# Decoder trunk step: one loop for three heads, sample mask built on VectorE, first transposes and loads of the attention moved forward

## The chip, the cores and the metric

The kernel runs on one core of one Trainium2 chip. The metric is the device time of one execution in microseconds (us). PE is the matrix engine (TensorE), DVE is VectorE, ACT is ScalarE, POOL is GpSimd and SP is SyncE, which here only issues DMAs.

## What is computed

One inference step of a two-layer decoder trunk, in float32, for a prompt (2048 tokens, width 1024) and for 8 sample sequences of 4 new tokens each with 2048 cached tokens. Both share the weights.

```python
# layer 0: gated linear attention (4 heads, dk 128, dv 256), chunks of 64 tokens
q, k, v, g, lr = split(rmsnorm(x) @ w_in)
log_a = log_sigmoid(lr @ w_a2 + b_a) / 16          # per token and key channel
b     = cumsum(log_a, within a chunk)
o     = tril((q*exp(b)) @ (k*exp(-b)).T) @ v + (q*exp(b)) @ S
S     = exp(b_last) * S + (k*exp(b_last - b)).T @ v
h     = x + (rmsnorm(o) * silu(g)) @ w_out
# layer 1: stick-breaking attention (16 heads of 64) on K, V made once from h
z     = q @ k.T / 8 + bias
w     = sigmoid(z) * product over later keys of (1 - sigmoid(z)), strictly causal
h     = h + ((w @ v) * silu(gate)) @ w_out2 ;  y = rmsnorm(h)
```

The outputs are y for both groups, the final states S, and K and V of all new tokens.

## The kernel before

The kernel is a row of stages, each a block in which every engine runs its own program and meets the others through semaphores; between blocks all engines meet. In order: the first projection (`proja`), the GLA stage (`gla`), its output projection (`outa`), the second projection (`projb`), the attention of the prompt (`att`), and the attention of the sample together with the last projection (`smp`).

**GLA.** The four heads follow one another. A head has 16 tiles of 128 prompt tokens and one tile of 32 sample tokens. The decay factors of the next head are made beside the tiles of the current one, in four spans of 512 tokens: PE multiplies `lr` by `w2` (L782, "logit"; L786 for the sample's 32 columns), DVE adds the bias (L945), DVE and ACT make the log-sigmoid (L953 to L957), DVE scans it into `b_sum` (L966), and so on. `order` is the list of the steps of a head; the first span's logit stands in its third tile. `first` is the list of what precedes head 0 and also makes head 0's factors. `over_heads` runs `first`, then heads 0 and 1 in a hardware loop with `h` in a register, then head 2 and head 3 written out, head 3 without the steps for a next head. `w2` and `bias` have one buffer each, so `gate_weights(h)` (L637) may only load them for a head when the fifth logit of the head before is copied (`logit_cp`). SP loads them for head 1 before its loop, and in head h, after the spans of the next head and three stores of `o`, those for head h+2 (L670 to L672). After that come the state store, the sample states out and in, two more stores of `o` and `sums` (L684).

The masks are made once. POOL sets and cuts `keep`, `tok_mask`, `row_mask`, `mask_work` and `smp_work` with affine selects (L973 to L1002). DVE casts `mask_work` and `smp_work` into the integer masks `may` and `may_smp` (L934, L935), which the predicated copies of the scores use (L881, L883). `smp_work` says which of the 32 sample tokens may look at which: the same sequence, and not later.

**Attention.** It goes over 8 pairs of heads, each in five phases, and in beats: `attention_schedule` writes the order out by hand, and every engine follows the same list. A "z" item makes the scores of one tile of queries for one head (PE), two sigmoids (ACT, L1638 and L1646), a product scan (DVE, L1688) and a product (POOL, L1721). The "first" phase puts two such items in each of beats 0 to 7, over 128 to 512 keys; from beat 8 one item of 1024 keys stands in a beat. An "a" item, from beat 11, transposes weights and multiplies by V. A "turn" item transposes 512 raw columns of K and of V (PE, L1612), copies K out (ACT, L1653) and V (DVE, L1697), and lets SP load the next raw tile and store K (L1471, L1522). `raw_k`, `raw_v` and `k_tok` have two buffers each, so turn m+2 needs what turn m has freed. For pair 0 the four turns stand at beats 7 to 10, for later pairs at beats 40 (pair - 1) + 12, +14, +16 and +18. With the turns of pair 0 SP also issues loads that are needed later: the K of span 3 and the Q of span 1, the Q of span 3, the K of pair 1 (8 transfers), and the sample inputs (`new.load`: page table, bias, and tokens in pieces of 128 bytes).

Of the kernel before, what the change touches and what calls it, by code (L numbers as in the profile page):

```python
# [24 lines left out]
ALU = mybir.AluOpType  # L25
# [7 lines left out]
P = 128  # L33
# [3 lines left out]
NSEQ, TSEQ = 8, 4  # L37
SMP = NSEQ * TSEQ
# [478 lines left out]
def gla(nc, c, projT, w_alpha2, b_alpha, state_in, state_prompt, state_sample, o_out, sums, early):  # L517
# [8 lines left out]
    with ExitStack() as stack:  # L526
# [23 lines left out]
        mask_work, smp_work = s.sb("mask_work", [P, P]), s.sb("smp_work", [SMP, NSEQ, TSEQ])  # L550
# [46 lines left out]
        def over_heads(engine, run):  # L597

            run(START, first)
            with engine.Fori(0, GH - 2) as h:  # L600
                run(h, order)
            run(GH - 2, order)
            run(GH - 1, [x for x in order if x[1] == 0])
# [23 lines left out]
        def _(sp):  # L627
# [31 lines left out]
            sp.wait_ge(logit_cp, 5)  # L659
            gate_weights(1)  # L660

            def run(h, is_last):
                for u in range(NCH):
                    if not is_last:

                        sp.wait_ge(o_mm, h * n_tiles + (n_tiles if u == NCH - 1 else 4 * u + 4))
                        span(h + 1, u)
                    if u < NCH - 1:
                        store_o(h, u)
                if not isinstance(h, int):  # L670
                    sp.wait_ge(logit_cp, h * 5 + 10)
                    gate_weights(h + 2)  # L672
# [12 lines left out]
            with sp.Fori(0, GH - 2) as h:  # L685
                run(h, False)
            run(GH - 2, False)
# [5 lines left out]
        def _(pe):  # L693
# [3 lines left out]
            def run(h, items):  # L697
# [52 lines left out]
                def sample():  # L750
# [10 lines left out]
                    pe.wait_ge(logit_cp, h * 5 + (5 if isinstance(h, int) and h == GH - 1 else 10))  # L761
# [103 lines left out]
        def _(dve):  # L865
# [7 lines left out]
            def run(h, items):  # L873
# [49 lines left out]
                for kind, off, *x in items:  # L923
# [8 lines left out]
                    elif kind == "masks":  # L932
                        dve.wait_ge(masks, 16)
                        dve.tensor_copy(may[:, :], mask_work[:, :]).then_inc(prep, 1)  # L934
                        dve.tensor_copy(may_smp[:, :], smp_work[:, :, :].rearrange("p s n -> p (s n)")).then_inc(prep, 1)  # L935
                        dve.wait_ge(prep, 6)
                    elif kind in ("logit", "logit_smp", "abs", "decay", "scan"):
# [22 lines left out]
                        else:  # L960
                            dve.wait_ge(log_sigmoid, span_no)
                            if h is START and u == 0:
                                dve.wait_ge(masks, 8)
# [7 lines left out]
        def _(pool):  # L971
# [6 lines left out]
            pool.memset(smp_work[:, :, :], 1.0).then_inc(masks, 1)  # L978
            pool.wait_ge(masks, 6)
# [12 lines left out]
            pool.affine_select(out=smp_work[:, :, :], in_=smp_work[:, :, :], compare_op=ALU.is_ge, fill=0.0,  # L992
                               base=0, pattern=[[-TSEQ, NSEQ], [0, TSEQ]], channel_multiplier=1).then_inc(masks, 1)
            pool.wait_ge(masks, 12)
            pool.affine_select(out=smp_work[:, :, :], in_=smp_work[:, :, :], compare_op=ALU.is_ge, fill=0.0,
                               base=0, pattern=[[TSEQ, NSEQ], [1, TSEQ]], channel_multiplier=-1).then_inc(masks, 1)
# [317 lines left out]
def attention_schedule():  # L1314
# [19 lines left out]
    def put(beat, item):  # L1334
        beside.setdefault(beat, []).append(item)
# [4 lines left out]
    for pair in range(PAIRS):  # L1340
        for m in range(4):
            put(7 + m if pair == 0 else 40 * (pair - 1) + LAG + 1 + 2 * m, ("turn", pair, m))
# [14 lines left out]
def prompt_attention(nc, c, projT, parts, b_sb, k_out, v_out, oT, new):  # L1357
# [48 lines left out]
    with ExitStack() as stack:  # L1406
# [34 lines left out]
        def _(sp):  # L1441
# [51 lines left out]
            load_first_k(1, 0, 4)  # L1493
            load_gate(0)
            for kind, pair, *x in order:
# [9 lines left out]
                elif kind == "turn":  # L1505
# [7 lines left out]
                    if pair == 0 and m == 0:  # L1513
                        load_first_k(3, 0, 4)
                        load_q(0, 1)
                    elif pair == 0 and m == 1:
                        load_q(0, 3)
                    elif pair == 0 and m == 2:
                        load_k(1)
                    elif pair == 0:  # L1520
                        new.load(sp)
# [828 lines left out]
```

## Time and profile before

| | |
|---|---|
| time, three runs | 3374.26 us median (3369.12 to 3375.23) |
| the profiled execution | 3375.23 us, span of its instructions 3373.6 us |
| PE busy | 3159.3 us, 94% of the span |
| DVE, ACT, POOL busy | 1661.7, 1398.5, 887.3 us |
| granted TensorE clock, mean | 0.969 of full speed |
| GLA stage | about 626 to 886 us |
| prompt attention | about 1888 to 2872 us |

An engine can only be late through its own queue: it works off its instructions in order, and one that waits holds all behind it. The busy share of PE says how much of the span could be taken from it at best; the waits in front of its instructions say where it stands.

### The profile page before, as it was taken

How to read it: one execution, taken by the hardware profiler on the slowest of the kernel's cores; microseconds unless marked ns; L12 is line 12 of the kernel's file. 1: busy time of each engine (PE TensorE's matmuls, PEld its weight loads, DVE VectorE, ACT ScalarE, POOL GpSimd, SP SyncE). 2: the span in 40 equal slices, each digit the busy share in tenths (PEclk: the TensorE clock that was granted, in tenths of full speed). 3: DMA queues.
4: the chain of work that ended last, by engine and by line, in shares of the span. 5: the costliest groups of instructions: out<-in, count | busy, mean ns of one | idle time of the engine just before them, and what ended most of it. 6: DMA issues, size and time to landing. Idle time of an engine off the chain costs nothing. (4 is left out here: it accounts for less than half of the span.)

```text
span 3373.6 us, 49748 instructions
## 1 busy us (share of the span) xinstructions
PE 3159.3 (94%) x17836; PEld 2480.2 (74%) x17836; DVE 1661.7 (49%) x1965; ACT 1398.5 (41%) x2330; POOL 887.3 (26%) x936
## 2 busy tenths in 40 slices
PE   6999999799799699999999589999999999799998
PEld 6999999556588599999999455555555555566665
DVE  5111122387444422112222288998999898443442
ACT  5111111365311221112211278888888787344442
POOL 0000000255111000000000256776767676000000
PEclk9999999799899899999999689999999999899999
DMA  4122111455254545213431455343433410899995
GB/s 152 57 75 75 69 57 58 165 180 184 101 175 147 178 158 181 76 68 133 175 101 44 135 162 136 77 125 113 110 97 100 126 32 20 348 323 375 368 336 212
DMA packets 253345, 489.74 MB, mean 145 GB/s; under 512 B 27181, under 2 KB 137490, under 8 KB 240850
## 3 DMA queue, kind: packets, MB, share of 16 engines
q1 hardware_dynamic: 228402, 350.61, 32.0%
q0 software_dynamic: 24752, 136.63, 11.3%
q8 instruction: 115, 1.88, 0.2%
q14 instruction: 76, 0.62, 0.1%
HBM read 329.58 MB, written 157.59 MB: 144 GB/s over the span
## 5 line engine op out<-in xcount | busy, mean ns | idle before, releaser
L1721 POOL TENSOR_TENSOR att_w<-att_w,att_rest 128x1023 f32<-128x1023 f32 (+7 forms) x384 | 614.7, 1604 | 303.1 <-DVE att_rest L1688 291.0
L469 PE MATMUL projb_acc<-projb_x_hi,projb_w_hi 128*128 128x416 f32 x1280 | 452.1, 353 | 25.9 <-DVE projb_x_lo L459 25.8
L469 PE MATMUL projb_acc<-projb_x_hi,projb_w_lo 128*128 128x416 f32 x1280 | 450.1, 352 | 0.0
L469 PE MATMUL projb_acc<-projb_x_lo,projb_w_hi 128*128 128x416 f32 x1280 | 449.6, 351 | 0.0
L1549 PEld LDWEIGHTS att_wT_acc<-const_ident,att_w 128*128 128x128 f32 x2176 | 237.0, 142 | 210.4 <-issue 153.1
L1638 ACT ACTIVATE att_rest<-att_z,att_bias 128x1024 f32<-128x1024 f32 (+7 forms) x384 | 332.9, 867 | 84.7 <-PE att_z L1595 36.4
L1688 DVE TENSOR_TENSOR_SCAN att_rest<-att_rest,att_zero 128x128 f32<-128x128 f32 (+7 forms) x256 | 355.0, 1402 | 22.9 <-ACT att_rest L1638 22.9
L292 PE MATMUL proja_acc<-proja_x_hi,proja_w_hi 128*128 128x416 f32 x1000 | 354.3, 354 | 0.8 <-DVE proja_x_lo L265 0.7
L292 PE MATMUL proja_acc<-proja_x_hi,proja_w_lo 128*128 128x416 f32 x1000 | 352.1, 352 | 0.0
L292 PE MATMUL proja_acc<-proja_x_lo,proja_w_hi 128*128 128x416 f32 x1000 | 350.3, 350 | 0.0
L1549 PE MATMUL att_wT_acc<-const_ident,att_w 128*128 128x128 f32 x2176 | 315.1, 281 | 31.1 <-ACT att_k_tok L1653 14.6
L1646 ACT ACTIVATE att_w<-att_z,att_bias 128x1024 f32<-128x1024 f32 (+7 forms) x384 | 331.9, 864 | 0.0
L1563 PE MATMUL att_o_acc<-att_wT,att_v_tok 128*64 128x512 f32 (+3 forms) x1280 | 305.3, 556 | 6.8 <-DVE att_silu L1706 5.9
L1688 DVE TENSOR_TENSOR_SCAN att_rest<-att_rest,att_carry,att_zero 128x1024 f32<-128x1024 f32 x128 | 299.2, 2337 | 7.1 <-ACT att_rest L1638 7.0
L418 ACT ACTIVATE projb_out<-projb_acc 128x416 f32<-128x416 f32 x160 | 83.1, 519 | 501.7 <-PE projb_acc L469 501.7
L230 ACT ACTIVATE proja_out<-proja_acc 128x416 f32<-128x416 f32 x125 | 64.5, 519 | 484.4 <-PE proja_acc L292 484.4
L469 PEld LDWEIGHTS projb_acc<-projb_x_hi,projb_w_hi 128*128 128x128 f32 x1280 | 241.2, 188 | 29.3 <-issue 19.6
L469 PEld LDWEIGHTS projb_acc<-projb_x_lo,projb_w_hi 128*128 128x128 f32 x1280 | 241.4, 189 | 3.2
L469 PEld LDWEIGHTS projb_acc<-projb_x_hi,projb_w_lo 128*128 128x128 f32 x1280 | 241.8, 189 | 2.2
L1676 DVE COPY att_wT<-att_wT_acc 128x512 f32<-128x512 f32 (+2 forms) x320 | 192.7, 602 | 93.1 <-PE att_wT_acc L1549 90.4
L1591 PE MATMUL att_z<-att_k,att_q_hi 128*128 128x512 f32 (+3 forms) x640 | 226.9, 420 | 0.4 <-ACT att_w L1646 0.4
L506 POOL DMA_DIRECT2D proj_b<-projb_out x32 | 17.1, 533 | 710.7 <-ACT projb_out L418 535.0
(256 smaller groups left out, 5066.4 us busy)
## 6 DMA issues: line engine op xcount, KB each, us to landing
smp_k_pages<-in_cache_k SPq DMA_DIRECT2D x128, 512.0 KB, 7.1
smp_v_pages<-in_cache_v SPq DMA_DIRECT2D x128, 512.0 KB, 7.2
proj_b<-projb_out POOLq DMA_DIRECT2D x32, 1040.0 KB, 4.4
proj_a<-proja_out POOLq DMA_DIRECT2D x24, 1040.0 KB, 4.5
kq_hi<-projb_slab POOLq DMA_DIRECT2D x16, 1024.0 KB, 6.0
kq_lo<-projb_slab POOLq DMA_DIRECT2D x16, 1024.0 KB, 8.9
att_q_hi<-kq_hi SPq DMA_DIRECT2D x60, 256.0 KB, 4.2
att_q_lo<-kq_lo SPq DMA_DIRECT2D x60, 256.0 KB, 5.1
```

The costliest lines, as they stand in the source:

```text
L230: act.activation(out[:, b, at:at + size], acc[:, q, 0:size], ACT.Sigmoid if gate else ACT.Copy).then_inc(copied, 1)
L292: mm = pe.matmul(acc[:, q, 0:size], w[:, b, k, :], x[:, k, at:at + size], start=(k == 0 and w is w_hi and x is x_hi), stop=(k == KD - 1 an ...
L418: act.activation(out[:, b, at:at + size], acc[:, q, 0:size], ACT.Sigmoid if kind == "gate" else ACT.Copy).then_inc(copied, 1)
L469: mm = pe.matmul(acc[:, q, 0:size], w[:, b, k, :], x[:, k, at:at + size], start=(k == 0 and w is w_hi and x is x_hi), stop=(k == KD - 1 an ...
L1549: mm = pe.transpose(wT_ps[:, h, (t % 4) * P:(t % 4 + 1) * P], weight(pair, phase, h, t, at, P), c.ident[:, :])
L1563: pe.matmul(o_ps[h * HD:(h + 1) * HD, lo:BANK], v_tok[:, pair % 2, j, h * HD:(h + 1) * HD], wT[:, h, n % 2, lo:BANK], start=(j == 4 * g + ...
L1591: pe.matmul(z_ps[:, n % 2, at:end], q_hi[:, t // 4, h, tile].bitcast(F32R), k2[:, pair % 2, h, lo + at:lo + end].bitcast(F32R), start=carr ...
L1638: act.activation(rest[:, n % n_rest, 1024 - size:1024], z_ps[:, n % 2, 0:size], ACT.Sigmoid, bias=bias[:, 1, head:head + 1], scale=-HD ** ...
L1646: act.activation(weight(pair, phase, h, t, 0, size), z_ps[:, n % 2, 0:size], ACT.Sigmoid, bias=bias[:, 0, head:head + 1], scale=HD ** -0.5 ...
L1676: dve.tensor_copy(wT[:, 1, n % 2, lo:BANK], wT_ps[:, 1, lo:BANK]).then_inc(copied[1], 1)
L1688: dve.tensor_tensor_scan(passing, passing, zero[:, 0:1].broadcast_to([P, size]), carry_of(t, h) if carried else rest[:, n % n_rest, 1024:1 ...
L1721: pool.tensor_tensor(these, these, passed[:, 1:size], ALU.mult).then_inc(w_made, 1)
```

## The change

There are three edits to the GLA stage and one to the attention. In GLA, the hardware loop now covers heads 0 to 2, and `gate_weights` for head h+1 is issued at the start of head h, for every head; `smp_work` and its selects are gone from POOL and `may_smp` is made on DVE from `tok_mask`, `row_mask` and `may`; the scan of the first span waits for all masks. In the attention, the turns of pair 0 stand at beats 4 to 7 and the loads that went with them are issued before the list begins.

```diff
         def over_heads(engine, run):
             run(START, first)
-            with engine.Fori(0, GH - 2) as h:
+            with engine.Fori(0, GH - 1) as h:
                 run(h, order)
-            run(GH - 2, order)
             run(GH - 1, [x for x in order if x[1] == 0])
...
             early.load(sp)
-            sp.wait_ge(logit_cp, 5)
-            gate_weights(1)
             def run(h, is_last):
+                if not is_last:
+                    sp.wait_ge(logit_cp, h * 5 + 5)
+                    gate_weights(h + 1)
                 for u in range(NCH):
...
-                if not isinstance(h, int):
-                    sp.wait_ge(logit_cp, h * 5 + 10)
-                    gate_weights(h + 2)
                 sp.wait_ge(s_made, h * NCK + NCK)
...
-            with sp.Fori(0, GH - 2) as h:
+            with sp.Fori(0, GH - 1) as h:
                 run(h, False)
-            run(GH - 2, False)
             run(GH - 1, True)
...
-                    pe.wait_ge(logit_cp, h * 5 + (5 if isinstance(h, int) and h == GH - 1 else 10))
+                    pe.wait_ge(logit_cp, h * 5 + (5 if isinstance(h, int) else 10))
...
                     elif kind == "masks":
-                        dve.wait_ge(masks, 16)
+                        dve.wait_ge(masks, 13)
                         dve.tensor_copy(may[:, :], mask_work[:, :]).then_inc(prep, 1)
-                        dve.tensor_copy(may_smp[:, :], smp_work[:, :, :].rearrange("p s n -> p (s n)")).then_inc(prep, 1)
+
+                        dve.wait_ge(prep, 5)
+                        dve.tensor_tensor(ke_smp[:, :, 0:SMP], tok_mask[0:SMP, :, :],
+                                      row_mask[:, :].unsqueeze(2).broadcast_to([SMP, NSEQ, SMP]), ALU.mult).then_inc(prep, 1)
                         dve.wait_ge(prep, 6)
+                        dve.tensor_reduce(mask_work[0:SMP, 0:SMP], ke_smp[:, :, 0:SMP].rearrange("p s n -> p n s"),
+                                      mybir.AxisListType.X, ALU.add).then_inc(prep, 1)
+                        dve.wait_ge(prep, 7)
+                        dve.tensor_tensor(mask_work[0:SMP, SMP:2 * SMP], mask_work[0:SMP, 0:SMP], may[0:SMP, 0:SMP],
+                                      ALU.mult).then_inc(prep, 1)
+                        dve.wait_ge(prep, 8)
+                        dve.tensor_copy(may_smp[:, :], mask_work[0:SMP, SMP:2 * SMP]).then_inc(prep, 1)
+                        dve.wait_ge(prep, 9)
...
                             if h is START and u == 0:
-                                dve.wait_ge(masks, 8)
+                                dve.wait_ge(masks, 13)
...
-            pool.memset(smp_work[:, :, :], 1.0).then_inc(masks, 1)
-            pool.wait_ge(masks, 6)
+            pool.wait_ge(masks, 5)
...
-            pool.affine_select(out=smp_work[:, :, :], in_=smp_work[:, :, :], compare_op=ALU.is_ge, fill=0.0,
-                               base=0, pattern=[[-TSEQ, NSEQ], [0, TSEQ]], channel_multiplier=1).then_inc(masks, 1)
-            pool.wait_ge(masks, 12)
-            pool.affine_select(out=smp_work[:, :, :], in_=smp_work[:, :, :], compare_op=ALU.is_ge, fill=0.0,
-                               base=0, pattern=[[TSEQ, NSEQ], [1, TSEQ]], channel_multiplier=-1).then_inc(masks, 1)
+            pool.wait_ge(masks, 10)
...
-            put(7 + m if pair == 0 else 40 * (pair - 1) + LAG + 1 + 2 * m, ("turn", pair, m))
+            put(4 + m if pair == 0 else 40 * (pair - 1) + LAG + 1 + 2 * m, ("turn", pair, m))
...
             load_raw(0, 0)
             load_raw(0, 1)
             load_first_k(1, 0, 4)
+            load_first_k(3, 0, 4)
             load_gate(0)
+            load_q(0, 1)
+            load_q(0, 3)
+            load_k(1)
+            new.load(sp)
...
-                    if pair == 0 and m == 0:
-                        load_first_k(3, 0, 4)
-                        load_q(0, 1)
-                    elif pair == 0 and m == 1:
-                        load_q(0, 3)
-                    elif pair == 0 and m == 2:
-                        load_k(1)
-                    elif pair == 0:
-                        new.load(sp)
```

## Rows read from the trace of the kernel before

**Rows 1.** Windows of busy time: stretch, length, busy per engine, clock, DMA share, GB/s.
```profile
626.00:886.00 260.00, 237.48 (x1284) 140.04 (x1284) 182.91 (x382) 134.18 (x373) 124.12 (x104) 0.91 0.53 179
...
1888.00:1960.00 72.00, 36.14 (x136) 24.83 (x136) 31.53 (x33) 30.82 (x53) 25.50 (x35) 0.57 0.80 204
...
660.00:664.00 4.00, 4.00 (x12) 1.70 (x13) 1.52 (x3) 0.75 (x3) 1.26 (x1) 0.66 0.00 0
...
1915.00:1920.00 5.00, 4.24 (x12) 2.12 (x12) 3.94 (x5) 4.12 (x9) 3.86 (x6) 0.50 0.10 25
```

**Rows 2.** Timeline, GLA: start, duration, PE's logits in heads 1 and 2.
```profile
718.86 1.12 PE L782 MATMUL gla_logit_acc<-gla_rT,gla_w 16*128 16x512 f32 x2
...
776.21 1.12 PE L782 MATMUL gla_logit_acc<-gla_rT,gla_w 16*128 16x512 f32 x2
```

**Rows 3.** Line L684 (store of sums), near 718 and 775: issue, landing.
```profile
L684 SPq DMA_DIRECT2D sums<-gla_sumsq_out x1: 890/890/890, 717.9 to 717.9; - x1
DMA to landing us min/median/max: 6.0/6.0/6.0
...
L684 SPq DMA_DIRECT2D sums<-gla_sumsq_out x1: 763/763/763, 775.1 to 775.1; - x1
DMA to landing us min/median/max: 5.6/5.6/5.6
```

**Rows 4.** Tile gla_w, whole span: from issue to landing of its four loads.
```profile
DMA to landing us min/median/max: 1.9/6.6/9.1
```

**Rows 5.** Timeline of PE in GLA: start, duration, idle before and its releaser.
```profile
659.98 1.12 PE L782 MATMUL gla_logit_acc<-gla_rT,gla_w 16*128 16x512 f32 x2 [1.55 <-DMA gla_w<-in_w_alpha]
...
766.46 0.66 PE L706 MATMUL gla_tok<-const_ident,gla_vgT 128*128 128x128 f32 x4
...
769.75 0.97 PE L706 MATMUL gla_tok<-const_ident,gla_vgT 128*128 128x128 f32 x4
...
823.91 0.66 PE L706 MATMUL gla_tok<-const_ident,gla_vgT 128*128 128x128 f32 x4
...
826.00 0.60 PE L706 MATMUL gla_tok<-const_ident,gla_vgT 128*128 128x128 f32 x4
```

**Rows 6.** Timeline, 630 to 644: the masks and what follows them.
```profile
630.02 0.14 POOL L1002 MEMSET gla_mask_work<- 64x64 f32 x1
...
636.94 0.16 DVE L935 CAST gla_may_smp<-gla_smp_work 32x32 int32<-32x32 f32 x1
...
639.43 1.60 DVE L957 SCALAR_TENSOR_TENSOR gla_logit<-gla_logit,gla_work 128x512 f32<-128x512 f32 x1 [2.33 <-ACT gla_work L842]
...
643.15 0.29 DVE L879 COPY gla_ke<-gla_kp 128x128 f32<-128x128 f32 x1 [1.45 <-PE gla_kp L714]
```

**Rows 7.** Tile gla_tok_mask: min/median/max ns, first and last start.
```profile
L891 DVE TENSOR_TENSOR gla_q_smp<-gla_qT,gla_tok_mask x4: 406/406/407, 700.5 to 867.7; 128x256 f32<-128x256 f32 x4
```

**Rows 8.** Waits, 1924.2 to 1957: us in total, times, longest.
```profile
ACT att_k_tok L1653 <- DMA out_k_prompt<-att_k_tok: 16.1, 3, 7.4
```

**Rows 9.** Timeline, 1908 to 1957: issues of SP and ACT's steps.
```profile
1908.97 0.63 SPq L1477 DMA_DIRECT2D att_silu<-proj_b  x1
...
1922.46 1.25 SPq L1465 DMA_DIRECT2D att_q_hi<-kq_hi  x2
...
1926.23 1.11 ACT L1638 ACTIVATE att_rest<-att_z,att_bias 128x1024 f32<-128x1024 f32 x1
...
1949.62 8.08 SPq L1522 DMA_DIRECT2D out_k_prompt<-att_k_tok  x1
...
1955.46 0.60 ACT L1653 ACTIVATE att_k_tok<-att_wT_acc 128x512 f32<-128x512 f32 x1 [4.93 <-DMA out_k_prompt<-att_k_tok]
1955.96 1.11 ACT L1638 ACTIVATE att_rest<-att_z,att_bias 128x1024 f32<-128x1024 f32 x1
```

**Rows 10.** The page, costliest groups: count, busy us, mean ns of one.
```profile
L1688 DVE TENSOR_TENSOR_SCAN att_rest<-att_rest,att_carry,att_zero 128x1024 f32<-128x1024 f32 x128 | 299.2, 2337 | 7.1 <-ACT att_rest L1638 7.0
```

**Rows 11.** Line L1477, 1907 to 1910: landing of the gate load.
```profile
DMA to landing us min/median/max: 7.9/7.9/7.9
```

More of the change, by code:

```diff
@@ L549, in gla @@
         may, may_smp = s.sb("may", [P, P], I32), s.sb("may_smp", [SMP, SMP], I32)
-        mask_work, smp_work = s.sb("mask_work", [P, P]), s.sb("smp_work", [SMP, NSEQ, TSEQ])
+        mask_work = s.sb("mask_work", [P, P])
         sumsq, sumsq_out = s.sb("sumsq", [P, n_tiles]), s.sb("sumsq_out", [P, n_tiles])
```

## The prediction

> **What bounds the kernel now.** I read the page's busy line first: TensorE (PE) is by far the busiest engine, so what counts is what makes it stand. The change touches only two short stretches, so next I read the windows by stage: gated linear attention (GLA, 626 to 886 us) and the first 72 us of the prompt attention [rows 1]. In the first, PE is busy 237.5 of 260 us: a wait put in front of PE there is paid in full. In the second PE is busy 36.1 of 72 us at a clock of 0.57 with the DMA engines 0.80 busy: this is a start-up bound by transfers. Then I read, around each edit, who waits for whom and when each transfer was issued and landed.
>
> **Part 1: the gate weights in GLA.** Before, SyncE issues the weights `w2` and the bias for head h+2 in the middle of head h, ahead of that head's stores. After, it issues those for head h+1 as the first thing of head h. For head 1 nothing changes. For heads 2 and 3 the load now stands behind the whole tail of the previous head: state store, sample states out and in, two stores of `o`, `sums`. The last of these, `sums`, is issued at 717.9 and at 775.1 and takes 0.9 and 0.8 us to issue [rows 3], so `w2` goes out at about 718.9 and 776.0. PE asks for it in the third tile of the head, at 718.86 and 776.21 [rows 2]. So the load leaves when it is already wanted, and every microsecond to its landing is a wait of PE, in whose queue all later matmuls of the head stand.
>
> How long is that? `sums` is only 8.5 KB and still lands 6.0 and 5.6 us after its issue, at 723.9 and 780.7 [rows 3], behind 1 MB of states each way and 0.5 MB of `o`. `w2` is next in the same queue. `w2` would follow them by a few tenths; but SyncE's tail also starts about 1 us earlier, since two issues are gone from in front of it, and some of that is kept. I take 723.9 and 780.6 for `w2` itself: 723.9 - 718.9 = 5.0 and 780.6 - 776.2 = 4.4, together 9.4 us of waiting. Bounds: 1.9 us from issue to landing, the shortest of these loads [rows 4], gives 1.9 + 1.7 = 3.6; `sums`'s own landing plus another 2 us each gives 13.4. The bias lands just behind `w2`, while the pair of matmuls runs (1.12 us [rows 2]), so VectorE's wait for it is hidden; uncovered it costs a few tenths.
>
> The Trainium skill (DMA: Bandwidth & Descriptors, Anatomy of one DMA) gives a fixed cost of about 2 us for a small transfer; by that alone the two waits would be about 4 us. The same page (Queues, rings and completion order) says descriptors of a ring are consumed in order and a completion count lands only after that engine's earlier writes; the 6.0 us of the 8.5 KB transfer agree with this.
>
> Then the clock. After a gap of only 1.55 us in front of an earlier logit matmul, the granted clock of the next 4 us was 0.66 [rows 1, 5]: PE fell to its 1.2 GHz level for a while. The price is read from one tile at either level: the first tile of head 2 takes 769.75 - 766.46 = 3.29 us in such a phase, that of head 3 takes 826.00 - 823.91 = 2.09 us at full clock [rows 5]. So 1.2 us per phase; I take 1.3 for each of two waits, 2.6 (from 0 to 2 x 2.5). Nothing later gives this back, since PE has little idle time in this stage to shrink [rows 1].
>
> **Part 2: head 2 in the loop.** The same instructions run, with one more jump back. No row prices a jump by itself, but the two heads' first logits, 57.35 us apart with an unrolled entry between them [rows 2], leave no room for a dear one either way: 0.4 us as an estimate, from 0 to 1.
>
> **Part 3: the masks.** GpSimd loses a memset and two selects, and the scan's wait for 13 instead of 8 is free, since GpSimd's last mask starts at 630.02 and VectorE casts, behind that scan, at 636.94 [rows 6]. VectorE gets five small operations where it had two, each waiting for the one before: product, reduction, product, two casts. The nearest row is a product of 128x256 at 406 ns [rows 7]; two of that size, three of 0.2 us, and the round trips between make about 2 us, up to 3.5 beside a busy GpSimd. Before, VectorE ends its casts at 637.1 and then idles 2.33 us for ScalarE and 1.45 us more before it copies the keys at 643.15 [rows 6]. That cover of 3.8 us hides it: 0. Without the cover it would cost 2 us once. What GpSimd saves is nothing either: it idles until the scan.
>
> **Part 4: the start of attention.** The turns (transposes of raw K and V) of pair 0 move from beats 7 to 10 to beats 4 to 7, and all loads that hung on them are issued in one go: the first K of span 3 (2 transfers), Q of spans 1 and 3 (8), K of pair 1 (8), and the sample inputs (table, bias, tokens). Before, ScalarE waits 16.1 us, in three pieces, for the stores of these turns [rows 8]. This looks like a prize. But turns 2 and 3 need raw tiles that are only loaded once turns 0 and 1 have freed their buffers; they now queue behind all of the list.
>
> Rate: between the issue at 1922.46 and ScalarE's release at 1955.46 there are 31 transfers of 256 KB in one queue, so about 1.0 us each after the queue filled [rows 9]. The gate load of 1908.97 landed 7.9 us later, at 1916.9 [rows 11]. After: 1916.9 + 18 = 1934.9; the sample inputs, cut in pieces of 128 bytes, add about 2.5: 1937.4. SyncE itself is held: in the before kernel the issue right behind them took 8.08 us, until 1957.75 [rows 9]. So the raw K of turn 2 leaves about 1936 and the raw V lands about 1940.3. PE meets turn 2 at about 1921 and stands until 1940; before, it did beats 7 to 10 in that time.
>
> From there: ScalarE's copy waits for the first store (1941.5), then four sigmoids of beat 7 at about 0.7 us (1.11 at twice the width [rows 9]), the copy of turn 3, and the first full-width sigmoid at 1945.4; it was at 1926.23 [rows 9]. Five such steps lie between it and the sixth: at VectorE's pace, 2.34 us for a scan [rows 10] and small copies beside it, 13.7 us with the turn. So the sixth starts at 1959.1, where it was at 1955.96 after three stalls [rows 9]: +3.1. From here before ran at half clock with gaps; a PE that has been kept busy for 14 us should not: -1.5. Sum +1.6. What comes back is the DMA engines' idle time, 0.10 busy from 1915 to 1920 where the stage's mean is 0.80 [rows 1]; what is lost is that PE no longer works in it. Bounds: raw V landing at 1934 (0.7 us a transfer) gives -5; the 8.08 us once more on top gives +9.
>
> **Sum.** 9.4 + 2.6 + 0.4 + 0 + 1.6 = +14.0 us. The profiled execution took 3375.23 (span 3373.6), 1 us over the median 3374.26. 3375.2 + 14.0 = 3389.
>
> **Rivals.** (A) Late transfers are not held by the backlog: the engines serve them beside the queued ones. Then `w2` costs 3.6 us, clock 1.2, jump 0.4, and raw V, issued at 1924, is there by 1927, which pulls the sixth step to 1945.7: -10. Sum -4.8: 3370, not slower. It decides once raw V lands before 1930. For: 0.10 DMA share at 1917. Against: an 8.5 KB transfer took 6.0 us. (B) Only the small loads slip past, or the tail of the head runs ahead, and the clock stays up: 3.6 + 0.4 + 1.6 = +5.6: 3381. (C) The scattered sample inputs hold SyncE longer than reckoned: +8 more, 3397; the 8.08 us issue speaks for it. (D) The early list drains at the higher rate: attention -5, sum +7.4: 3383.
>
> **How the numbers follow.** Forecast as summed, 3385 to 3394: 0.56. A 0.10, B 0.12, C 0.12, D 0.10. A measurement of this kernel tells about 0.2% (6.7 us) from no change: slower starts at 3381. Slower: the forecast, C, half of B and most of D, 0.80. Same: half of B, most of A, some of D, 0.14. Faster: a tail of A, 0.06. Range 3378 to 3398: it leaves out A and the tails of C.
>
> **What would show it.** In the profile after: the first logit matmul of heads 2 and 3 with about 5 us of idle, released by the DMA of `w2`, and a dip of the granted clock behind it; the GLA stage longer by some 12 us; about 1.5 to 2.5 us of mask work on VectorE with the first key copy no later; no rows of turns between 1921 and 1940 and PE idle there, released by raw K or V; DMA share near 1 from 1900 to 1946 without a gap. It is wrong if `w2` lands within 2 us, or if the turns of beat 6 do not wait.

## The result and the profile after

The change makes the kernel slower: 3396.92 us (median of 4, 3391.98 to 3398.95) against 3374.74 us (median of 4) of the kernel before on the same chip, ratio 1.0066, 95% interval 1.0049 to 1.0085. That is +22.2 us between the medians. The profiled execution took 3394.23 us with a span of 3392.6; the traces so compare at 3392.6 - 3373.6 = +19.0 us. The forecast was +14.

Where the 19.0 us lie is found by marks in both traces. The GLA stage, from its first to its last transposition of keys, takes 240.7 us in place of 221.7: +19.0. The first projection ended 2.0 us sooner, the second took 1.3 us more and the gap in front of it 1.3 us more; these and smaller differences cancel. The attention, from its first scores to its last gate, takes 976.1 us in place of 977.6. So all of it is the GLA stage. (A gate is the product L1706 of a finished piece of output with its `silu` factor; there are 32.) One trace against another is coarse: with the same GLA code the stage takes between 215.9 and 223.8 us, as the table of experiments shows. Windows of the whole stage, after (stretch, length, busy time of each engine, clock, DMA share, GB/s):

```profile
626.00:886.00 260.00, 237.06 (x1251) 139.57 (x1252) 180.60 (x372) 132.49 (x369) 119.71 (x93) 0.88 0.52 172
```

Against [rows 1] PE has the same busy time but fewer matmuls (1251 records, not 1284) and a clock of 0.88, not 0.91. That is how such a loss looks in a window: the busy share does not fall, since a matmul at half clock counts as busy for longer. The window is also fixed while the stage has grown, so it holds less of the stage's work. PE's waits in the stage from 640 us on, after (total, times, longest):

```profile
PE gla_logit_acc L778 <- DMA gla_w<-in_w_alpha: 11.7, 3, 6.3
```

PE's timeline at the first logit of heads 0, 1 and 2; they answer to [rows 5] and [rows 2]:

```profile
658.23 1.12 PE L778 MATMUL gla_logit_acc<-gla_rT,gla_w 16*128 16x512 f32 x2 [1.48 <-DMA gla_w<-in_w_alpha]
...
722.62 2.07 PE L778 MATMUL gla_logit_acc<-gla_rT,gla_w 16*128 16x512 f32 x2 [3.86 <-DMA gla_w<-in_w_alpha]
...
788.75 2.07 PE L778 MATMUL gla_logit_acc<-gla_rT,gla_w 16*128 16x512 f32 x2 [6.32 <-DMA gla_w<-in_w_alpha]
```

The two last rows had no wait before. Their own duration has gone from 1.12 to 2.07 us: the clock is down as they run. SyncE's timeline shows why the weights are late:

```profile
708.71 3.14 SPq L641 DMA_DIRECT2D gla_s_in<-in_state_gla  x1
712.11 3.15 SPq L646 DMA_DIRECT2D o_gla<-gla_o  x1
715.44 1.16 SPq L679 DMA_DIRECT2D o_gla<-gla_o_smp  x1
716.84 0.92 SPq L681 DMA_DIRECT2D sums<-gla_sumsq_out  x1
718.32 0.35 SPq L637 DMA_DIRECT2D gla_w<-in_w_alpha  x1
```

The load is issued at 718.32 and PE starts at 722.62, 4.3 us later. From issue to landing, the load itself and then the store of `sums` that stands in front of it, both heads:

```profile
DMA to landing us min/median/max: 4.2/4.5/4.8
...
L681 SPq DMA_DIRECT2D sums<-gla_sumsq_out x2: 344/630/917, 716.8 to 783.0; - x2
DMA to landing us min/median/max: 5.5/5.5/5.5
```

So `sums` lands at 722.3 and 788.5 and `w2` about 0.2 us behind it, both times.

The clock behind the first of the two long waits (2 us a window; PE's busy time is the second figure):

```profile
720.00:722.00 2.00, 0.00 (x0) 0.00 (x0) 0.00 (x0) 0.31 (x2) 1.26 (x1) 0.74 0.29 84
722.00:724.00 2.00, 1.39 (x2) 0.50 (x2) 0.00 (x0) 0.00 (x0) 0.00 (x0) 0.50 0.00 0
724.00:726.00 2.00, 2.00 (x7) 0.63 (x8) 0.75 (x1) 0.22 (x1) 0.00 (x0) 0.50 0.00 0
726.00:728.00 2.00, 2.00 (x7) 1.06 (x6) 0.96 (x2) 0.53 (x3) 0.00 (x0) 0.50 0.00 0
728.00:730.00 2.00, 2.00 (x12) 1.53 (x10) 0.43 (x3) 1.07 (x2) 0.00 (x0) 0.50 0.00 0
730.00:732.00 2.00, 2.00 (x10) 0.95 (x7) 1.12 (x3) 0.79 (x4) 1.63 (x1) 0.70 0.12 24
```

PE is busy throughout from 722.62 but at 0.50, the 1.2 GHz level, for more than 8 us. What the low clock loses is PE's busy time in a window times one minus the clock: 1.39 x 0.5 + 6 x 0.5 + 2 x 0.3 = 4.3 us. The same sum behind the wait of head 2 gives 3.7 us, together 8.0. One head can be closed to 0.1 us. From logit to logit it is 788.75 - 722.62 = 66.13 us, 8.8 more than the 57.35 of [rows 2]. Into it fall the wait of 6.32 us and the 4.3 us of clock, and out of it a phase at the low level that the kernel before had near 766 to 771, 1.7 us by the same sum: 6.3 + 4.3 - 1.7 = 8.9.

The masks, VectorE's timeline after, beside [rows 6]:

```profile
634.83 0.20 DVE L930 CAST gla_may<-gla_mask_work 128x128 int32<-128x128 f32 x1
635.07 1.25 DVE L933 TENSOR_TENSOR gla_ke_smp<-gla_tok_mask,gla_row_mask 32x256 f32<-32x256 f32 x1
636.35 0.59 DVE L936 TENSOR_REDUCE gla_mask_work<-gla_ke_smp 32x32 f32<-32x256 f32 x1
636.98 0.52 DVE L939 TENSOR_TENSOR gla_mask_work<-gla_mask_work,gla_may 32x32 f32<-32x32 f32 x1
637.53 1.17 DVE L942 CAST gla_may_smp<-gla_mask_work 32x32 int32<-32x32 f32 x1
638.74 0.69 DVE L964 SCALAR_TENSOR_TENSOR gla_logit<-gla_logit,gla_work 128x512 f32<-128x512 f32 x1
...
641.54 0.29 DVE L875 COPY gla_ke<-gla_kp 128x128 f32<-128x128 f32 x1 [1.46 <-PE gla_kp L710]
```

It is 3.9 us of work where it was 0.3. The operation that follows has no idle time in front of it, where VectorE stood 2.33 us for ScalarE, and the wait in front of the first copy of keys is what it was (1.46, before 1.45).

The attention's first turns, PE and ScalarE, and the issue that holds them:

```profile
1960.57 1.11 PE L1610 MATMUL att_wT_acc<-const_ident,att_raw_k 128*128 128x128 f32 x4 [18.69 <-DMA att_raw_k<-proj_b]
```
```profile
1962.09 0.60 ACT L1651 ACTIVATE att_k_tok<-att_wT_acc 128x512 f32<-128x512 f32 x1 [19.94 <-DMA out_k_prompt<-att_k_tok]
...
1966.12 1.11 ACT L1636 ACTIVATE att_rest<-att_z,att_bias 128x1024 f32<-128x1024 f32 x1
```
```profile
1944.58 0.59 SPq L1741 DMA_DIRECT2D new_tokens<-proj_b  x1
1945.28 12.76 SPq L1473 DMA_DIRECT2D att_raw_k<-proj_b  x1
1958.08 0.43 SPq L1473 DMA_DIRECT2D att_raw_v<-proj_b  x1
```

The attention starts 20.8 us later in this trace. In the terms of the kernel before, PE meets the third turn with its data at 1939.8 and the first full-width sigmoid stands at 1945.3.

### The profile page after: what moved, and what is told of

Same layout as the page of the kernel before. It is cut to its first block and busy times, and to the rows that moved or that the text cites. A ratio compares the mean times of both kernels' runs of the same rounds, so it can differ in the third digit from the quotient of the medians.

```text
span 3392.6 us, 50001 instructions
## 1 busy us (share of the span) xinstructions
PE 3158.6 (93%) x17836; PEld 2475.2 (73%) x17836; DVE 1664.0 (49%) x1968; ACT 1398.7 (41%) x2330; POOL 887.5 (26%) x933
## 5 line engine op out<-in xcount | busy, mean ns | idle before, releaser
L469 PEld LDWEIGHTS projb_acc<-projb_x_hi,projb_w_hi 128*128 128x128 f32 x1280 | 241.3, 188 | 32.1 <-issue 21.2
L469 PEld LDWEIGHTS projb_acc<-projb_x_lo,projb_w_hi 128*128 128x128 f32 x1280 | 241.3, 189 | 3.2
```

What stands on the lines that cost most here:

```text
L469: mm = pe.matmul(acc[:, q, 0:size], w[:, b, k, :], x[:, k, at:at + size], start=(k == 0 and w is w_hi and x is x_hi), stop=(k == KD - 1 an ...
```

## The experiments

Twelve kernels were run in four groups, each beside the kernel before on the same chip. "GLA" and the gates are from the trace of the profiled execution: the length of the stage as above, and the time from the first scores of the attention to its first and last gate. The four groups ran on different chips, so between groups the ratios compare and not the medians. The traces have noise of their own: the attention as it was before reaches its first gate after 74.3 to 77.8 us and its last after 977.5 to 981.1 (before, g1, g2, g4, g5, g6).

| kernel | median us | ratio to before, 95% | GLA | first gate | last gate |
|---|---|---|---|---|---|
| before | 3374 to 3378 | 1 | 221.7 | 74.3 | 977.6 |
| after | 3396.92 | 1.0066 [1.0049, 1.0085] | 240.7 | 74.4 | 976.1 |
| g1_loop_and_weights | 3395.14 | 1.0047 [1.0031, 1.0064] | 242.8 | 74.4 | 977.5 |
| g2_weights_at_start | 3396.70 | 1.0054 [1.0038, 1.0071] | 241.3 | 75.7 | 979.0 |
| g3_weights_back | 3380.28 | 1.0008 [0.9998, 1.0018] | 216.1 | 74.7 | 976.4 |
| g4_filler | 3393.27 | 1.0051 [1.0032, 1.0071] | 238.0 | 76.4 | 979.6 |
| g5_behind_states | 3391.34 | 1.0039 [1.0025, 1.0054] | 235.2 | 77.8 | 981.1 |
| g6_filler5 | 3394.48 | 1.0054 [1.0041, 1.0068] | 240.9 | 74.8 | 978.0 |
| a1_attention_only | 3377.01 | 1.0001 [0.9991, 1.0010] | 215.9 | 76.0 | 977.8 |
| a2_front_turns7 | 3377.36 | 1.0002 [0.9992, 1.0013] | 223.8 | 74.1 | 975.7 |
| a3_turns4_late | 3374.53 | 0.9993 [0.9983, 1.0003] | 223.5 | 58.4 | 973.1 |
| b1_spread | 3358.99 | 0.9946 [0.9933, 0.9960] | 220.2 | 59.0 | 960.8 |
| b2_spread_w2 | 3354.35 | 0.9933 [0.9921, 0.9945] | 216.7 | 58.5 | 961.8 |
| b3_masks | 3355.11 | 0.9936 [0.9920, 0.9952] | 216.8 | 60.7 | 962.3 |

**Which edit.** g1_loop_and_weights is the kernel before with the two GLA edits alone, the loop over three heads and the weights at the head's start. g2_weights_at_start leaves the loop as it was and moves only the weights:

```diff
-            sp.wait_ge(logit_cp, 5)
-            gate_weights(1)
...
             def run(h, is_last):
+                if not is_last:
+                    sp.wait_ge(logit_cp, h * 5 + 5)
+                    gate_weights(h + 1)
...
-                if not isinstance(h, int):
-                    sp.wait_ge(logit_cp, h * 5 + 10)
-                    gate_weights(h + 2)
```

> The kernel before with only the loop over heads 0 to 2 and the gate weights issued at the start of a head. Theory 1 (late weights): in the changed kernel PE waited 3.9 and 6.3 us for w2 and the period of heads 1 and 2 grew by 9.5 and 8.2 us, the rest being a half-speed clock behind each wait; so this kernel is 17 to 19 us slower than before, about 3392. Theory 2 (the GLA edits explain only their waits, about 10 us, and the rest of the loss sits in the masks or the attention): 3384 to 3386.

> The kernel before with the gate weights issued at the start of a head, the loop as it was (heads 0 and 1 in the loop, head 2 written out). Theory 1: the place of the loads is the whole cause, the same 17 to 19 us as with the loop, about 3392, and the two waits of 4 to 6 us in the same places. Theory 3 (the third pass of the loop costs by itself, through its jump or the fetch of its instructions): 4 us or more faster than the kernel with both edits, 3388 or less.

Both cost what the whole change costs, as far as their intervals tell, and g2 without the loop no less than g1 with it: the loop is worth nothing that can be measured (the intervals are some 5 us to either side), and the new place of two small loads is the loss. g3_weights_back is the opposite: the changed kernel, with this diff and the loop undone and everything else kept.

> The changed kernel with only its GLA loop and gate weights put back as before; the masks on VectorE and the attention's edits stay. Theory 1: all of the loss is gone, 3372 to 3375, and it equals the kernel with the attention's edits alone within 1 us, so that the masks cost nothing. Rival (the masks cost 1 us or more): later than that kernel by this much, seen in the start of the first key copy after the first projection.

Its ratio spans 1, so masks and attention together cost nothing that can be measured; the upper end of the interval is 6 us. The closer expectations were missed: 3380.28 us lies above 3372 to 3375 and 3.3 us above a1_attention_only, not within 1. Ten times of each kernel spread over 12 to 13 us, so these times can't settle a cost of 1 to 3 us for the masks; b3_masks below does. a1_attention_only has the attention's two edits on top of the kernel before.

> The kernel before with only the attention's edits: turns of pair 0 at beats 4 to 7, all loads in front. In the changed kernel the stage ended 1.4 us less late than it began. Theory 1 (one long wait of PE, 18.7 us, replaces three shorter ones and is about paid by them): 0 to -3 us, 3372 to 3375. Rival (the edit costs time, as the forecast had it with +1.6, or more through SyncE held behind the sample inputs): +2 to +8 us, 3376 to 3382.

Also no change: 1.0001, or 0.4 us below the kernel before on the same chip, which had a median of 3377.4.

**What the wait consists of.** g4_filler is g2 with unread matmuls in the place of the wait. PE then works through the time in which it would stand:

```diff
+                        if h is not START and u == 0:
+                            pe.wait_ge(logit_cp, h * 5 + 5)
+                            for _ in range(8):
+                                pe.matmul(logit_ps[:, :], c.ident[:, :], keep[:, 0:BANK], start=True, stop=True)
                         pe.wait_ge(ld["w2"], h * 16 + (16 * off + 16))
```

> The gate weights at the start of a head as in the kernel of that name, and before the wait for w2 in front of a head's first logit PE runs 8 matmuls of 512 columns whose result nobody reads (about 3.5 us). Nothing else changes. Theory (half of the loss is not the wait but the half-speed clock after it, about 4 us after the first wait and 3 after the second): the clock stays up in heads 1 and 2, 5 to 8 us come back there; in head 0, where the wait was only 1.5 us, the filler costs 2 us. Net 3 to 6 us faster than the kernel without it. Rival (the slow phase does not depend on what PE does while it waits): no gain in heads 1 and 2, 2 us slower in all.

PE's timeline and the clock behind it, g4_filler:

```profile
720.22 7.03 PE L775 MATMUL gla_logit_acc<-gla_keep,const_ident 128*128 128x512 f32 x16
727.19 1.12 PE L783 MATMUL gla_logit_acc<-gla_rT,gla_w 16*128 16x512 f32 x2
```
```profile
726.00:728.00 2.00, 2.00 (x5) 0.48 (x3) 0.00 (x0) 0.00 (x0) 0.00 (x0) 1.00 0.00 0
728.00:730.00 2.00, 2.00 (x12) 0.94 (x12) 1.20 (x2) 0.75 (x3) 0.00 (x0) 1.00 0.00 0
```

The logit takes 1.12 us again and the clock stays at 1.00. Eight matmuls took 7.03 us, twice what was expected (the row counts 16, two for each float32 matmul). The fillers stand in heads 0, 1 and 2 and take 3 x 7.03 = 21.1 us, where g2 waited 1.77, 6.70 and 4.89 us for `w2`, 13.4 us in all. The stage should be 7.7 us longer and is 3.3 us shorter (238.0 against 241.3). So 11.0 us came back. By the sum of the windows, g2 loses 3.4, 3.5 and 3.1 us behind its three waits, 10.0 us together, and g4 nothing there; 1.4 us more lies in front of the first filler and has nothing to do with it. This is the price of the second half of the wait, 3.3 us each, taken with no wait left. It is seen in the traces alone. The two kernels' times do not tell them apart (1.0051 and 1.0054), since longer fillers eat up most of the gain.

g6_filler5 has five such matmuls, not eight.

> g2_weights_at_start with five unread matmuls of 128x512 instead of eight before each first logit of heads 1 to 3. Eight took 7.0 us and kept the clock at 1.00, in a wait of 5.5 to 6.7 us. If the clock's fall is worth 3 to 4 us a wait, as the windows of the kernel after say: five take 4.4 us, a short wait of 1 to 2 us stays, the clock stays up or dips for a moment, GLA 5 to 7 us shorter than in g2, 3389 to 3392. If a wait of 1 us behind the fillers is enough to drop the clock, as 1.55 us was before: 2 to 3 us shorter at most, 3393 to 3395.

The second reading held (3394.48 us; the stage is 0.4 us shorter than in g2). In head 0 the five fillers cover the wait and nothing is lost. In head 1 PE waits only 2.58 us behind 4.46 us of fillers, and that suffices:

```profile
723.93 1.61 PE L783 MATMUL gla_logit_acc<-gla_rT,gla_w 16*128 16x512 f32 x2 [2.58 <-DMA gla_w<-in_w_alpha]
```
```profile
724.00:726.00 2.00, 2.00 (x6) 0.52 (x6) 0.42 (x1) 0.00 (x0) 0.00 (x0) 0.61 0.00 0
726.00:728.00 2.00, 2.00 (x9) 0.83 (x6) 0.55 (x2) 0.75 (x3) 0.00 (x0) 0.50 0.00 0
728.00:730.00 2.00, 2.00 (x9) 1.71 (x8) 0.73 (x2) 0.21 (x1) 0.00 (x0) 0.50 0.00 0
```

A short wait costs nearly as much clock as a long one: 3.4 us here by the same sum and 3.2 behind the 2.16 us of head 2, against 3.5 and 3.1 in g2. This is why a wait of 4 to 6 us is worth 8 to 10.

**What makes the load late.** g5_behind_states leaves the weights in the tail of the head before, but puts them behind the sample states instead of ahead of all the tail:

```diff
-                if not isinstance(h, int):
-                    sp.wait_ge(logit_cp, h * 5 + 10)
-                    gate_weights(h + 2)
...
                 if not is_last:
                     sample_states(h + 1)
+                if not isinstance(h, int):
+                    sp.wait_ge(logit_cp, h * 5 + 10)
+                    gate_weights(h + 2)
```

> The kernel before with the gate weights for head h+2 one step later in the tail of head h: behind the sample states out and in (2 MB) and ahead of the stores of o. They are issued about 712.8, six us before PE asks at 718.9. Theory (the queue holds a small load behind what was issued before it: the states in landed at 722.2): PE still waits about 3.4 us twice and pays the clock, 8 to 14 us slower than before. Rival (what matters is only that the load leaves 2 us or more before it is wanted; the weights then land by 715): no wait, within 2 us of before.

SyncE's issues, the landing of the states and then of `w2` (both heads), and PE's logit, g5_behind_states:

```profile
710.21 2.78 SPq L642 DMA_DIRECT2D gla_s_in<-in_state_gla  x1
713.27 3.27 SPq L638 DMA_DIRECT2D gla_w<-in_w_alpha  x1
```
```profile
L642 SPq DMA_DIRECT2D gla_s_in<-in_state_gla x2: 2781/3079/3377, 710.2 to 774.4; - x2
DMA to landing us min/median/max: 11.8/11.9/12.0
```
```profile
DMA to landing us min/median/max: 8.5/8.7/8.9
```
```profile
722.30 1.77 PE L782 MATMUL gla_logit_acc<-gla_rT,gla_w 16*128 16x512 f32 x2 [3.58 <-DMA gla_w<-in_w_alpha]
```

The states land at 722.0 and 786.4 us, and `w2`, issued 3.1 and 3.6 us behind them, 0.1 to 0.2 us later. So the landing is set by the states ahead of the load, not by when it is issued. Against the changed kernel `w2` leaves 5.05 us earlier in head 1 (713.27 against 718.32) and 5.85 in head 2 (778.02 against 783.87), and lands 0.3 and 2.2 us earlier; the waits are 3.58 and 3.66 us in place of 3.86 and 6.32. Most of the loss stays: 1.0039, or 15.7 us, slightly above the 8 to 14 that were expected. Of the three places that were run only the one ahead of the states makes the loads free, where the kernel before has them.

**The attention.** a2_front_turns7 issues all the loads in front, but leaves the turns at beats 7 to 10. a3_turns4_late has the turns at beats 4 to 7, and the same loads only behind the fourth turn:

```diff
-            put(7 + m if pair == 0 else 40 * (pair - 1) + LAG + 1 + 2 * m, ("turn", pair, m))
+            put(4 + m if pair == 0 else 40 * (pair - 1) + LAG + 1 + 2 * m, ("turn", pair, m))
...
+                    if pair == 0 and m == 3:
+                        load_q(0, 1)
+                        load_first_k(3, 0, 4)
+                        load_q(0, 3)
+                        load_k(1)
+                        new.load(sp)
```

> The kernel before with all loads of the attention in front of its list, the turns of pair 0 left at beats 7 to 10. Theory (the list in front is what PE waits for at the third turn; two more beats of work stand ahead of that turn here, so the wait shrinks from 18.7 us to about 11): 3 to 6 us faster than before. Rival (the place of the turns does not matter, since the same loads must pass the queue before anything goes on): within 1 us of the kernel with both edits.

> The kernel before with the turns of pair 0 at beats 4 to 7 and the loads that are needed later (Q of spans 1 and 3, K of span 3, K of pair 1, sample inputs) issued only behind the fourth turn. Theory (raw tiles and stores then go through an empty queue, and the 18.7 us wait of the changed kernel and the 14.5 us of waits of the one before both vanish): 9 to 13 us faster than before, no wait of ScalarE for a store of K in the first 70 us of the stage. Rival (the loads put off collide with the turns of pair 1 and the second span's Q, and the waits come back there): 0 to 4 us faster.

a2 is no change, and the 3 to 6 us that were expected did not come: loads in front neither help nor harm where the turns come late. For a3 the rival held: it is 1.1 us faster than the kernel before on its chip, with a ratio that spans 1, and not 9 to 13. It reaches the first gate 16 us sooner (58.4 against 74.3 us), but is only 2.9 us ahead at the second gate and at all others up to the 29th. Its chain of waits, 1950 to 2002, shows where the rest went, into the turns of pair 1:

```profile
ACT att_k_tok L1650 <- DMA out_k_prompt<-att_k_tok: 13.3, 1, 13.3
...
PE att_wT_acc L1609 <- DMA att_raw_k<-proj_b: 11.1, 1, 11.1
```
```profile
1953.35 0.59 SPq L1740 DMA_DIRECT2D new_tokens<-proj_b  x1
1954.04 10.20 SPq L1471 DMA_DIRECT2D att_raw_k<-proj_b  x1
```

The raw load that pair 1 needs takes 10.20 us to issue, right behind the tokens in their pieces of 128 bytes; behind them stood the issue of 12.76 us in the changed kernel and of 8.08 us before [rows 9]. The wait had only been handed on. b1_spread keeps those loads away from every turn that waits:

```diff
+                    if pair == 0 and m == 3:
+                        load_q(0, 1)
+                        load_first_k(3, 0, 4)
                     if m == 3:
                         sp.dma_start(v_out...)
+                    if pair == 0 and m == 3:
+                        load_q(0, 3)
+                    elif pair == 1 and m == 1:
+                        load_k(1)
+                    elif pair == 1 and m == 3:
+                        new.load(sp)
```

> The kernel before, with the turns of pair 0 at beats 4 to 7, but with the large loads spread out: Q of span 1 and K of span 3 behind the raw loads and in front of the V store of the fourth turn, Q of span 3 behind that store, the K of pair 1 only behind the second turn of pair 1, and the sample inputs only behind the fourth turn of pair 1. Theory (the turns need only a free road for their raw tiles; the 13 us lost in a3_turns4_late are the raw loads of pair 1 standing behind K of pair 1 and the sample inputs): the first gate 14 to 16 us earlier than before, no wait of 10 us in the turns of pair 1, and the later gates keep 12 to 16 us of it; 3359 to 3364. Rival (something else holds the later gates, for example K or Q of the next pair): the first gate early, the later ones 0 to 4 us early as in a3_turns4_late, 3371 to 3376.

It held, and slightly better: 3358.99 us, 0.9946 of the kernel before. The first gate is 15.3 us early, and so is every gate up to the 29th; the last three are 16.8 early, the difference being a phase at the low clock that the kernel before has at 2784 to 2788 us, far behind the edit. Among the waits above 3.2 us between 1946 and 2000 none is left for a raw tile or for a store of `k_tok`.

**The one wait that was left in GLA.** b2_spread_w2 is b1 with the first head's weights ahead of the six early loads:

```diff
-            early.load(sp)
             sp.wait_ge(logit_cp, 5)
             gate_weights(1)
+            early.load(sp)
```

> b1_spread, and in GLA the gate weights of head 1 are issued ahead of the six early loads instead of behind them. If a wait of 1.55 us costs its length and a phase at the 1.2 GHz level behind it: the wait in front of the first logit of head 0 is gone and GLA is 3 us shorter, 1.5 of wait and 1.5 of clock. Rival: the clock falls there anyway, or the six early loads, now 5 us later, hold the tiles of head 0: 0 to 1.5 us, or slower.

Held: the stage is 3.5 us shorter (216.7 against 220.2). In b1 the logit of head 0 waits 1.59 us and the next 4 us run at 0.58, which loses 1.7 us; in b2 both are gone. The medians, from one chip, differ by 4.6 us. The windows from 660 to 664, b1 and then b2:

```profile
660.00:664.00 4.00, 4.00 (x13) 1.70 (x12) 1.71 (x3) 0.75 (x3) 0.84 (x1) 0.58 0.00 0
```
```profile
660.00:664.00 4.00, 4.00 (x28) 2.84 (x29) 3.02 (x8) 2.20 (x7) 1.78 (x2) 1.00 0.46 160
```

PE is busy for 4.00 us in both, with 13 matmuls in one and 28 in the other.

**The masks alone.** b3_masks is b2 with the mask edit of the change, as in its diff.

> b2_spread_w2 with the sample mask made on VectorE and GpSimd's smp_work gone, as in the changed kernel: the mask edit by itself. Theory (3.9 us of mask work on VectorE lie in the time in which it would wait for ScalarE and the keys): the first keys of head 0 come no later after the first projection's end, GLA within 0.5 us of its length, 3352 to 3357, with before at about 3376. Rival (GpSimd, 3 operations lighter, lets the first keys come earlier): the stage starts 1 to 1.5 us sooner, 3350 to 3354, which these rounds can hardly tell. Other rival: the five operations wait for each other and for GpSimd's last mask and push the keys out by 1 to 2 us: 3356 to 3358.

3355.11 us, and b2 3354.35; the ratios are 0.9936 and 0.9933: no difference that these runs can tell. The stage has the same length to 0.1 us; the first transposition of keys stands 24.4 us behind the end of the projection, in b2 23.9.

## Why the prediction was near, and where it was off

Sign and range were right, and so were the sum of the two waits in GLA and the long wait in the attention; the middle was 8 us low (5 us against the profiled execution). That it was not lower still is partly luck: two terms were too low and one too high. By its steps:

1. The wait for `w2`, 5.0 + 4.4 = 9.4 us: measured 3.86 + 6.32 = 10.2. The sum is nearly right, its split is not. In head 1 PE asks at 718.76 and the load goes out at 718.32, 0.4 us before, where I had them together; in head 2 PE asks at 782.43, 1.4 us ahead of the issue at 783.87, where I had the issue 0.2 us ahead. `w2` landed 0.2 us behind `sums`, as I had argued. That the small load is bound by what is ahead of it is shown by g5, where it lands 0.1 to 0.2 us behind the states though it was issued 5.05 and 5.85 us earlier than in the changed kernel. The Trainium skill (DMA: Bandwidth & Descriptors, Anatomy of one DMA) gives a fixed cost of about 2 us, for DMAs issued by GpSimd, while these are SyncE's. By that alone the waits would have been about 4 us. Measured is 4.2 and 4.8 us from issue to landing behind the states; the 1.9 us of the shortest load [rows 4], the first of the stage, are the only ones near the page's figure. Its section Queues, rings and completion order has descriptors consumed in ring order, and g5 agrees.
2. The clock, 1.3 us a wait: **this is the term that was mis-sized.** It measured 4.3 and 3.7 us in the trace, and 3.3 a wait by g2 and g4. I had read the price from one tile, 3.29 against 2.09 us [rows 5], as if the phase were one tile long. But that phase followed no wait of the kind to be priced, and behind the waits it lasted more than 8 and 7 us. The bound I had kept, 2.5 us a wait, did not reach it. It makes 5.4 us of the difference. The Trainium skill (TensorE: Matmul & The Clock Gate, Terms) puts the penalty at the time at the low level times one minus the clock's ratio. The traces agree: over the stage that sum is 11.4 us lower in g4 than in g2, and the lengths of the stages, the fillers and the waits give 11.0.
3. The loop, 0.4 us: g1 against g2 shows no cost.
4. The masks, 0: right, though the work is 3.9 us and not 2 to 3.5. I had reckoned one product of 128x256 at 406 ns as the price of one on 32x256; it took 1.25 us, while GpSimd worked beside it (its product L1024 starts at 635.00 us). Of the 3.6 us more, 0.4 reach the keys: from the scan to the first copy of keys it is 7.85 us after and 7.45 in b2, which has the old masks. b3 shows by itself that no more comes of it.
5. The attention, +1.6 us: it measured +0.1 at the first gate and at all gates to the 29th, and -1.5 at the last three. The last 1.6 us are not the edit's: they are the phase at the low clock that the trace of the kernel before has at 2784 to 2788 us and the one after has not. Nor can +1.6 be told from +0.1, since the first gate varies by 3.5 us between traces of one attention code, and stands at 76.0 in a1. Shifted by 20.8 us, the third turn was forecast at 1940 and stood at 1939.8, the first full-width sigmoid at 1945.4 and stood at 1945.3. The sixth was forecast at 1959.1 and came at 1956.8, so the steps between were reckoned too slow; from there to the first gate 0.7 us came back, where I had put 1.5 down to the clock. That the gain of beats 4 to 7 goes into one long wait for the raw tiles is shown by a3 and b1: without the loads in front there is no such wait, and the first gate comes 16.0 and 15.3 us sooner.

Against the profiled 19.0 us the forecast's 14.0 so miss +5.4 of clock behind the waits, +1.7 from a longer phase at the low level before them (706 to 714 us), +0.8 of wait, +0.4 of masks, -0.4 of the loop and -3.1 of attention: 4.8 of the 5.0. The parts in GLA by themselves were forecast at 12.4 us and measured 19.0; the attention's term, of which 1.6 us is the phase far behind the edit, covered part of this.

Rivals A and B are out: small transfers do not slip past the queued ones (g5). Rival C, SyncE held by the sample inputs, did come about in size (12.76 us where 8.08 were known), but the turn came when the forecast had it. That the measured 3396.9 us is also C's number, 3397, is chance: the loss lies in GLA, and a1 and the marks show none of 8 us in the attention. Rival D is out, the turn came when the forecast said. Neither condition stated as showing the prediction wrong occurred: `w2` took 4.2 and 4.8 us, and the third turn waited 18.69.

What stays open: why the stage has phases at the low level that follow no wait of PE for `w2` (706 to 716 us after, 708 to 714 before). They are worth 1.7 or 3.4 us each. The stage differs by 7.9 us between traces of the same GLA code (215.9 in a1, 223.8 in a2). In a1 there is no phase at all between 656 us and the stage's end. a2 has two that follow no wait, 3.4 us together, one of 3.4 behind a wait of 2.16 us, and the wait is 1.5 us longer: 8.3. g3 has no phase either, and before has three, 5.1 us in all, one of them behind its wait of 1.55 us. In a1 and g3 the wait for `w2` in head 0 was 0.69 and 0.76 us, in all others with head 1's weights in the old place 1.37 to 2.16. That shorter wait can't be all that spared them: b2 and b3 have no wait in head 0, and each still has a phase of 1.7 us from 816 on.

## What to carry to other kernels

Here the small load, issued behind bulk transfers, landed 0.1 to 0.3 us behind the last one ahead of it (after, g1, g2 and g5), so its place in the order of issue mattered more than its time of issue. Put such a load ahead of bulk stores and loads, even if its buffer has to come free earlier. When TensorE runs at full clock, price a wait as its length plus what the clock loses behind it, and read the second from a wait of the same kind; here it was 2.9 to 4.3 us behind every wait of 1.77 us or more. When a stall is removed by moving work forward, look for the next consumer of the same queue: a3 moved 13 of 16 us to pair 1, and only spreading the bulk loads (b1) kept them.

## What the runs showed of the hardware

- What the clock loses behind a wait of PE for `w2` hardly grows with the wait. By the sum used above it lost nothing behind waits of 0.69 and 0.76 us, 1.7 us behind 1.37, 1.48, 1.55 and 1.59 us, and 3.2 to 3.4 us behind 1.77, 2.01, 2.07, 2.16 (twice), 2.58, 3.58 and 3.66 us, though PE was busy all the time that followed. Behind 3.86 us it was 4.3, more than the wait, but behind 4.89, 4.91, 6.32, 6.70 and 7.03 us it was 3.1, 2.9, 3.7, 3.5 and 3.1.
- The fillers of g4, 7.03 us in the place of waits of 1.77 to 6.70 us, kept the clock at 1.00 and cost nothing but their own time.
- An issue of SyncE can be held for long. The one right behind the tokens took 8.08, 10.20 and 12.76 us, where the issues of one large transfer from 1927 to 1946 us in the kernel before take 0.33 to 0.63 us, and the tokens' own issue 0.59. It need not be the tokens' small pieces: in b1 the issue behind them took 3.45 us for two transfers, and with no tokens near, issues of b1 at 1935.19 took 7.32 us for two and those of the GLA tail behind the states 2.8 to 3.9 us. Which of the two, the pieces or the transfers still queued, makes the length was not tried.
- A product of 32x256 took 1.25 us and a cast of 32x32 1.17 us on VectorE while GpSimd was busy, against 0.16 us for the cast of the old mask [rows 6], in front of which GpSimd stood still. In the kernel before, the step L957 on 128x512 took 0.69 us at 634.97 with GpSimd idle and 1.60 us at 639.43 [rows 6] with GpSimd busy. Whether GpSimd is the reason was not tried.
